# A memory key projection before the first norm, weights one block behind their modulation, and three products on a cleared area

## What is computed

```python
mod = silu(c) @ w_ada + b_ada                    # six vectors of 2048
h = rms_norm(x, norm1_g) * (1 + scale1) + shift1
lru_x, lru_gate, q, k, v, g_a, g_b = split(h @ w_in)
xc = causal_depthwise_conv(lru_x, conv_w, conv_b)   # 4 taps along the sequence
...
for l in range(2):                               # the hybrid layers
    k_mem, v_mem = split(mem @ w_mem_kv[l])      # depends on no other layer
    y_mem = attention(mq, k_mem, v_mem)          # 4 heads of 128
    x = layer_norm(ALPHA * x + concat(y_fox, y_dsa, y_mem) @ w_out[l])
```

## Time and profile before

| | us |
|---|---|
| median of 3 runs (2656.99 to 2657.73) | 2657.61 |
| the profiled execution, whole time | 2657.43 |
| its span, first to last instruction | 2655.4 |

### The profile page before, as it was taken

The page is one execution under the profiler, slowest core; times in us unless marked ns, Lnnn a source line. Parts: engine busy times, 40 slices in busy tenths (PEclk is TensorE's granted clock), DMA queues, the critical chain, the costliest instruction groups (busy, mean ns, idle before and its releaser), DMA issues.

```text
span 2655.4 us, 35562 instructions
## 1 busy us (share of the span) xinstructions
PE 2634.3 (99%) x13776; PEld 2229.6 (84%) x13776; DVE 1843.5 (69%) x2522; ACT 1376.2 (52%) x2028; POOL 77.1 (3%) x134
## 2 busy tenths in 40 slices
PE   8999999999999999999999999999999999999998
PEld 7888877777888888888888888888888888888886
DVE  7876788887888776655665566776566667764665
ACT  4137766654444664455445545544554565445543
POOL 0000000000000000000000000100010001000000
PEclk9999999999999999999999999999999999999999
DMA  9985578788989586655565565565546746655463
GB/s 387 409 334 167 172 261 273 264 287 294 333 313 345 199 303 206 198 191 182 193 200 192 184 206 173 180 204 180 165 142 193 230 164 192 212 179 167 145 221 129
DMA packets 164568, 595.34 MB, mean 224 GB/s; under 512 B 19360, under 2 KB 20416, under 8 KB 163888
## 3 DMA queue, kind: packets, MB, share of 16 engines
q1 hardware_dynamic: 158544, 574.00, 63.5%
q0 software_dynamic: 5856, 19.06, 2.3%
HBM read 584.53 MB, written 3.21 MB: 221 GB/s over the span
## 4 chain that ended last, share of the span: by engine, by line
PE 90%; DVE 4%; ACT 2%; DMA 2%; issue 1%; SPq 0%; DVEq 0%; ACTq 0%
PE bank L834 27%; PE bank L876 26%; PE bank L888 14%; PE bank L839 13%; PE pX L945 1%; PE pS L922 1%; PE bank L851 1%; DVE both_w L1641 1%; PE bank L817 1%; DMA raw<-in_w_x 1%; PE pX L934 1%; ACT both_w L1203 1%; DVE XC L2146 1%; DMA raw<-in_w_vw 1%; PE pS L851 1%
## 5 line engine op out<-in xcount | busy, mean ns | idle before, releaser
L1641 DVE TENSOR_TENSOR both_w<-raw,both_w 128x1024 fp32r<-128x1024 f32 x848 | 1023.3, 1217 | 535.2 <-ACT both_w L1203 531.3
L1203 ACT ACTIVATE both_w<-raw 128x1024 fp32r<-128x1024 f32 x848 | 881.2, 1050 | 604.9 <-PE bank L839 356.9
L876 PE MATMUL bank<-H,both_w 128*128 128x512 f32 x3232 | 777.3, 391 | 0.2 <-DVE XC L2146 0.2
L876 PEld LDWEIGHTS bank<-H,both_w 128*128 128x128 f32 x3232 | 592.7, 188 | 117.6 <-issue 2.9
L888 PE MATMUL bank<-H,both_w 128*128 128x256 f32 x3232 | 440.1, 285 | 1.4 <-DVE both_w L1641 1.4
L888 PEld LDWEIGHTS bank<-H,both_w 128*128 128x128 f32 x3232 | 420.1, 191 | 22.5 <-DVE both_w L1641 2.1
L834 PE MATMUL bank<-both_w,H 128*128 128x512 f32 x1152 | 291.3, 395 | 6.9 <-ACT both_w L1203 6.9
L834 PEld LDWEIGHTS bank<-both_w,H 128*128 128x128 f32 x1152 | 214.9, 189 | 55.4 <-ACT both_w L1203 7.6
L834 PE MATMUL bank<-both_w,F 128*128 128x512 f32 x1024 | 253.0, 389 | 0.0
L1693 DVE SCALAR_TENSOR_TENSOR raw<-raw,CR 128x1024 f32<-128x1024 f32 x192 | 232.3, 1218 | 16.3 <-DMA raw<-in_ada 15.5
L834 PEld LDWEIGHTS bank<-both_w,F 128*128 128x128 f32 x1024 | 192.1, 188 | 40.0
(11 more groups left out here) (326 smaller groups left out, 2375.5 us busy)
## 6 DMA issues: line engine op xcount, KB each, us to landing
raw<-in_w_in SPq DMA_DIRECT2D x296, 512.0 KB, 3.5
raw<-in_w_ff SPq DMA_DIRECT2D x256, 512.0 KB, 4.1
raw<-in_ada SPq DMA_DIRECT2D x192, 512.0 KB, 5.5
raw<-in_w_out SPq DMA_DIRECT2D x96, 512.0 KB, 4.6
raw<-in_w_sig SPq DMA_DIRECT2D x64, 512.0 KB, 4.9
raw<-in_w_vw SPq DMA_DIRECT2D x48, 512.0 KB, 4.3
raw<-in_w_x SPq DMA_DIRECT2D x32, 512.0 KB, 15.1
raw<-in_w_lru_out SPq DMA_DIRECT2D x32, 512.0 KB, 4.8
```

Source lines behind the costliest of these rows:

```text
L876: ins = pe.matmul(out[i].rearrange("p (a s) -> p a s", a=2), whi[:, s, at_:at_ + 128], both[:, :, kt, :], start=(c == 0 and k == 0), stop= ...
L1203: act.activation(whi[:, s, 0:el.n], raw[el.slot][:, 0:el.n], ACT.Copy).then_inc(s_hi, 1)
L1641: dve.tensor_tensor(wlo[:, s, 0:n], raw[el.slot][:, 0:n], v32(whi[:, s, 0:n]), ALU.subtract).then_inc(s_lo, 1)
```

## The change

- A third `pre` unit computes `km` 3 (second key half of the second layer) in the front, as a mode "f" unit of 4 chunks; `km` 3 leaves the third norm. The result goes through a staging area to DRAM and is fetched into KM by GpSimd's queue beside the values.
- Its four weight tiles stand in the stream between the last four modulation tiles of block 1.
- In group 8 of the stream two blocks' weights are loaded (6 and 7); from there on weights are one block behind their modulation.
- VectorE clears 512 columns of SQ at the start and TensorE does three products of 512 columns on them before its first chunk.
- Counts and thresholds follow.

```diff
     for l in range(2):
         unit("pre", l, "vw", l, "MS", **whole)
+    unit("pre", 2, "kv", 3, "MS")
@@
         if l == 0:
-            for j in range(2):
-                unit("km", 2 + j, "kv", 2 + j, "M1")
+            unit("km", 2, "kv", 2, "M1")
@@
-    while first:
+    for c in range(4):
+        weight(early[2], c)
         modulation(*first.pop(0))
@@
         for c0 in (16, 0):
-            weight(parts.pop(0), 0)
+            for _ in range(2 if b == 8 else 1):
+                weight(parts.pop(0), 0)
             columns(c0 + b)
@@
-                due += 0 if n < 96 or 268 <= n < 290 else 0.5 if n < 152 else 0.72
+                due += 0 if n < 100 or 272 <= n < 294 else 0.5 if n < 156 else 0.72
@@
             if un.part == "open" and un.j == 0:
-                un.after = ("pre", 2)
+                un.after = ("pre", 3)
@@
-        if un.kind in ("q", "k"):
+        if un.kind in ("pre", "q", "k"):
             return EB
@@
-                            pe.wait_ge(s_ev["km"], 2 * l + job.b + 1)
-                            pe.wait_ge(s_vmr, 16 * (l + 1))
+                            pe.wait_ge(s_ev["km"], 3 if l else job.b + 1)
+                            pe.wait_ge(s_vmr, 48 if l else 16)
@@ TensorE, before its first unit
+        pe.wait_ge(s_vc, 1)
+        for i in range(3):
+            pe.matmul(pS2[:, i % 2, :], SQ[:, 0:128], SQ[:, 0:512], start=True, stop=True, skip_group_check=True)
@@ ScalarE, leaving a unit
-            if kind == "pre" and j == 1:
+            if kind == "pre" and j == 2:
                 norm1(0)
-                act.activation(STAGE[j][:, :, :], bank[:, un.bank:un.bank + 2, :], ACT.Copy).then_inc(s_ev["pre"], 1)
+                act.activation(STAGE[j], ps[:, :] if j == 2 else bank[:, un.bank:un.bank + 2, :], ACT.Copy).then_inc(s_ev["pre"], 1)
@@ VectorE, before its first unit
+        vc.add(dve.memset(SQ[:, 0:512], 0.0))
@@ GpSimd
+                    pool.dma_start(keys_d, STAGE[2]).then_inc(s_vst, 16)
@@
                         pool.dma_start(VM[:, :, :], values_d[l]).then_inc(s_vmr, 16)
+                        if l:
+                            pool.dma_start(pair(KM, 1), keys_d).then_inc(s_vmr, 16)
```

More of the change, by code:

```diff
@@ L307, in _plan @@
         if un.kind == "pre":
-            un.ahead = [min(i, order[15]) for i in un.ahead]
+            un.ahead = [min(i, order[19]) for i in un.ahead]
         elif un.part and un.part != "close":
@@ L508, in _build @@
     CT = [at("CT0", [128, CH], o_pt), at("CT1", [128, CH], o_lp + 1024)]
-    STAGE = [at("STAGE0", [128, 2, 512], o_pt), at("STAGE1", [128, 2, 512], o_tg + 4096)]
+    STAGE = [at("STAGE0", [128, 2, 512], o_pt)[:, :, :], at("STAGE1", [128, 2, 512], o_tg + 4096)[:, :, :],
+             at("STAGE2", [128, 512], o_tg + 2048)[:, :]]
     SQ = at("SQ", [128, CH], o_tg)
@@ L550, in _build @@
     values_d = nc.dram_tensor("values", (2, 128, 2, 512), F32, kind="Internal").ap()
+    keys_d = nc.dram_tensor("keys", (128, 512), F32, kind="Internal").ap()
     gates_d = nc.dram_tensor("gates", (2, NB, 128), F32, kind="Internal").ap()
@@ L2373, in gpsimd @@
                     pool.wait_ge(s_sp, 2)
-                    pool.wait_ge(s_ev["pre"], 2)
+                    pool.wait_ge(s_ev["pre"], 3)
                     for l in range(2):
-                        pool.dma_start(values_d[l], STAGE[l][:, :, :]).then_inc(s_vst, 16)
+                        pool.dma_start(values_d[l], STAGE[l]).then_inc(s_vst, 16)
+                    pool.dma_start(keys_d, STAGE[2]).then_inc(s_vst, 16)
                     for c in (0, 3, 1, 2):
                         if c == 1:
-                            pool.wait_ge(s_vst, 32)
+                            pool.wait_ge(s_vst, 48)
                         pool.dma_start(LW[c][:, :], d_lru[c]).then_inc(s_lw, 16)
```

## The result

The changed kernel takes 2665.17 us in the median of 7 runs (2664.71 to 2666.49); the kernel before, on the same chip, 2657.49 us (7 runs, 2656.99 to 2657.73). The ratio is 1.003, with a 95% interval of 1.0021 to 1.004: slower by 7.7 us, 0.9 us more than was forecast. The profiled execution took 2666.06 us with a span of 2664.1, so 8.7 us more span than before; the traces are compared by that.

A forecast was written before the change was run, and what follows sets the result against it. TensorE, busy 2634.3 of 2655.4 us, was taken as the bound, with loads setting the pace in late `lrux`. 6.6 + 9.1 + 2.8 - 0.4 - 11.2 = +6.9 us on 2657.43 gave 2664.3 us, range 2659.5 to 2668.0.

The forecast's parts named there:

- The stand: Ahead of q: the first q unit gets banks 2 and 3, so TensorE waits 9.4 us for `conv(3)`, +9.1 us.
- The front: Up to the end of `lrux`: the moved unit adds 11.2 us, 4.6 us of waits are eaten up, +6.6 us.
- Held slots: Late `lrux` loads: slots held longer, loads slip 1 to 2 us at tile (12,0), 1.3 covered; taken as 0.
- rival 4: Late `lrux` loads slip or VectorE's sum empties their queue: 1.5 to 3.5 us more, 2665.8 to 2667.8 us; chance 0.12.
- The clock at q: After the wait ahead of q, TensorE starts at 1.2 GHz, +2.8 us, priced from the program's first chunks.
- The unit, -11.2 in the third norm: Third norm: without `km` 3, `mq` starts earlier with its inputs ready in time, a full gain of 11.2 us.
- the split's -0.4: Third q unit: its wait for VectorE's split goes, since VectorE is 9 us ahead, -0.4 us.
- The three products: Start of kernel: they save up to 2.8 us in first chunks, lost to a longer wait at chunk 11; 0.
- Rival 3: Start of kernel: the 2.8 us saved in the first chunks survive past chunk 11, 2661.5 us; chance 0.07.
- the sum by the rule of the Trainium skill alone: Whole kernel: if activity lifting the throttle were all that counted, the sum would be 2.8 us lower.
- Rival 2: Start of q: its first bank pair is free at `conv(1)` as before, no wait, 2652.8 us; chance 0.07.

The follow-up runs named there:

- turn_alone: Kernel before with only the first q unit put on banks 2 and 3: 2668.01 us, ratio 1.0039.
- ring: Changed kernel with loads on 12 slots only from group 15 on instead of 13: 2662.99 us, ratio 1.002.
- turn_two_behind: Changed kernel with the first q unit back on banks 0 and 1 and weights two blocks behind throughout: 2652.18 us, ratio 0.998.
- no_products: Changed kernel without the cleared area and the three products: 2663.93 us, ratio 1.0025.
- stand_filled: Changed kernel with 40 unread products of 512 columns in TensorE's wait ahead of q: 2662.66 us, ratio 1.002.
- lag_alone: Kernel before with only the weights one block behind their modulation from group 8 on: 2659.56 us, ratio 1.0008.
- q_turn: Changed kernel with the first q unit back on banks 0 and 1: 2654.02 us, ratio 0.9989.

## Why the prediction was right, and where not

- **The stand: right in place, cause and size.** 9.4 us were forecast from 0.3, 9.21 came from 0.16. The step that decided was to follow the count of units to the bank pair and from there to `("lrux", 4)`. turn_alone shows it without the rest of the change, and three pairs of kernels price the turn with its clock and split at 10.4 (turn_alone), 10.7 (ring) and 11.1 us (the changed kernel); my terms made 9.1 + 2.8 - 0.4 = 11.5.
- **The front: mechanism right, size off.** Forecast +6.6 at the close of half 0, measured +10.05. The failed step is "Held slots": I weighed tile (12,0) against a slip of 1 to 2 us, found 1.3 us of cover and took 0. By the list of loads, (12,0) takes the slot of a modulation tile 17 loads ahead and waits for no half. The binding tile was (12,1), which takes the slot of (10,1), 12 loads ahead: it stopped the in-order queue from 136.5 to 145.15, with block 13's modulation behind it. `norm1(15)` started at 170.66 instead of 167.6, 3.1 us late, TensorE waited 2.0, and the clock added 1.7. ring and turn_two_behind each remove the late tile, which settles the cause. That is rival 4 in its mechanism, with 3.7 us where it said 1.5 to 3.5; the median, 2665.17, fell between forecast and rival. A smaller misreading had no effect: `lrux` of the kernel before starts at 58.06 and not 58.2, so 4.8 us of waits were there to be eaten.
- **The clock at q: right that it falls, size off.** Forecast +2.8 from the start of the program; 1.4 in the changed kernel, 1.8, 2.1 and 2.7 in no_products, ring and turn_alone. The row that I took is the upper end. The 3.7 us of idleness ahead of the fall in the earlier trace rows is no fixed figure either: in the two stands of 9 us it was 2.1 and 5.1. stand_filled shows that it is the clock. The Trainium skill (TensorE: Matmul & The Clock Gate, Part 1) says that activity lifts the throttle and idleness brings it back, and that the number of slow products differs between runs of one kernel. The traces agree with the first: the clock is at half rate in the empty stand and at full rate in the filled one. The prices of 1.4 to 2.7 us stand each in one profile of another kernel, so for the second no run here shows more than that they differ. By these two misses, +3.45 in front and -1.4 here, and because the median lies 0.9 us under the profiled execution, the forecast hit the median more closely (0.9 us) than its terms deserve. That is luck.
- **The unit, -11.2 in the third norm, the split's -0.4: right.** `km` 2 starts at 2137.45 instead of 2117.60, and `mq` at 2152.35, where `km` 3 started at 2132.51: both moved by 19.8 us, so `mq` takes the place of `km` 3 without a loss. TensorE's waits between 2100 and 2200 are 0.2 us in all, before and after.
- **The three products at 0: right, by another road.** I expected the gain of 2.8 to turn into one wait of about 3 us at chunk 11. The fourth chunk starts at 15.29 instead of 17.95, 2.7 us ahead; then three waits take 0.73, 0.57 and 0.80 us where one took 0.36, and the rest goes in smaller delays; chunk 11's low products start at 42.30 instead of 42.51. Rival 3, and with it the sum by the rule of the Trainium skill alone, is out: the rule holds at the first chunk (2.90 us instead of 5.28), but it speaks of TensorE's pace and not of the end of a kernel, and the front isn't bound by TensorE there.
- **Not foreseen:** that weights one block behind cost 2.0 us by themselves (lag_alone). I checked that no weight and no modulation tile comes too late, not what one long wait does to the clock.
- **Rival 2** (no stand) was put at 2652.8; the kernels without the stand and the late tile came to 2652.2 to 2652.3. As a price for the version that keeps q on its old banks it was right.

What stays open: why q_turn's runs lie in two groups, seven at 2653.83 to 2654.59 and four at 2655.32 to 2656.96. A clock that falls at (15,0) in some executions and not in others would give a distance of 1.7 us, and the four lie 1.3 to 2.9 us above the median; no profile of the upper group was seen.

## What to carry to other kernels

A resource that is dealt out by a running count (banks by turns, buffers by rounds) changes hands for everything behind an added item: follow the count to the next user, and ask what frees its new share; here two lines turned a loss of 7.7 us into a gain of 3.5. A queue that issues in order stops as a whole at its first held buffer, so work out for each item of a narrower round when its slot comes free and what stands behind it, not only for the one that is due soonest. And compare each part of a change by itself: one part carried all the gain here, and was enough.

## What the runs showed of the hardware

- TensorE's granted clock fell from 2.4 to 1.2 GHz after a wait of 2.0 us in the changed kernel, and after 4.0 us in lag_alone, 0.8 and 1.3 us after the products had started again (means of 0.54 in 172 to 173 and 0.70 in 164 to 165); it held at 1.00 through waits of 1.54, 1.68 and 1.69 us at the same place (no_products, stand_filled, q_turn). From the end of the trace I hadn't expected a fall after so short a wait.
- In stands with no product at all it fell 2.1 us (changed kernel) and 5.1 us (turn_alone) behind the last product, and 3.7 us at the end of the program before.
- The price of one such fall lay between 1.4 and 2.7 us: 1.7 at (15,0) twice, 1.4, 1.8, 2.1 and 2.7 at q's start. The slow first chunks of the program before, with no fall ahead of them, cost 2.8.
- The products ahead of the first chunk took 4.50 us for six records, 0.75 us each, and the chunk behind them 2.90 us instead of 5.28.
